# LN1 output transposed by the DMA engines, and its passes laid out anew: an encoder block on eight cores

## The reference

```
x   = _layernorm(ALPHA * x + mix, ln1_g, ln1_b)        # x1, (tokens, 1024)
hid = square(relu(einsum('bsd,df->bsf', x, w_ff1)))    # (tokens, 4096)
ffn = einsum('bsf,fd->bsd', hid, w_ff2)
x   = _layernorm(ALPHA * x + ffn, ln2_g, ln2_b)
```

## Time and profile before

| | before |
|---|---|
| median of 3 runs | 1169.84 us (1169.5 to 1170.7) |
| profiled execution, its time | 1169.95 us |
| its span (first to last instruction, slowest core) | 1168.4 us; the eight cores 1162.7 to 1168.4 us |
| TensorE busy | 1135.6 us (97% of the span), 5594 matmuls |
| VectorE / ScalarE / GpSimd busy | 520.6 / 272.6 / 140.8 us |
| mean granted TensorE clock | 0.995 |

### The profile page before, as it was taken

The page is one execution under the profiler, slowest core; times in us unless marked ns, Lnnn a source line. Parts: engine busy times, 40 slices in busy tenths (PEclk is TensorE's granted clock), DMA queues, the critical chain, the costliest instruction groups (busy, mean ns, idle before and its releaser), DMA issues.

```text
span 1168.4 us, 15456 instructions; the slowest of 8 cores (1162.7 to 1168.4 us)
## 1 busy us (share of the span) xinstructions
PE 1135.6 (97%) x5594; PEld 521.7 (45%) x5594; DVE 520.6 (45%) x741; ACT 272.6 (23%) x417; POOL 140.8 (12%) x259
## 2 busy tenths in 40 slices
PE   6999999999999999999999999999999999999996
PEld 2544444444444444444444444444444444444442
DVE  0554465322248434503188445642222854442347
ACT  1224422211125333100011343221111443330000
POOL 4002200000011010100120121000000101000012
PEclk9999999999999999999999999999999999999998
DMA  9986776355552484764447438544334307444402
GB/s 131 179 139 121 141 134 112 48 81 81 91 90 46 66 125 74 111 120 75 73 85 180 105 88 169 104 83 76 63 66 81 60 0 124 83 83 73 73 37 108
DMA packets 30602, 110.36 MB, mean 94 GB/s; under 512 B 3648, under 2 KB 4160, under 8 KB 30016
## 3 DMA queue, kind: packets, MB, share of 16 engines
q0 software_dynamic: 24624, 88.36, 46.9%
q1 hardware_dynamic: 5904, 21.02, 5.9%
HBM read 189.33 MB, written 8.39 MB: 169 GB/s over the span
## 4 chain that ended last, share of the span: by engine, by line
PE 83%; DMA 8%; DVE 4%; issue 3%; ACT 1%; POOL 1%; DVEq 0%; ACTq 0%; SPq 0%; POOLq 0%
PE ps L263 83%; DMA ring<-wblk 4%; DMA t<-bsrow 2%; DMA xhTs<-xhT 2%; DVE regQ L757 1%; DVE regQ L834 1%; ACT regP L761 1%; POOL ring L144 1%; DVE regP L509 0%; PE ps L266 0%; DVE t L492 0%; POOL regR L144 0%; DVE t L504 0%; ACT t L488 0%; DVE Cc L472 0%
## 5 line engine op out<-in xcount | busy, mean ns | idle before, releaser
L263 PE MATMUL ps<-regR,ring 128*128 128x512 bf16 x2944 | 661.8, 379 | 14.2 <-DMA regR<-xT 7.0
L263 PEld LDWEIGHTS ps<-regR,ring 128*128 128x128 bf16 x2944 | 285.4, 98 | 354.8 <-issue 22.4
L263 PE MATMUL ps<-ring,regP 128*128 128x512 bf16 x1024 | 221.3, 379 | 0.9 <-ACT t L805 0.9
L144 POOL DMA_DIRECT2D ring<-wblk x145 | 77.5, 540 | 770.7 <-PE ps L263 766.7
L263 PEld LDWEIGHTS ps<-ring,regP 128*128 128x128 bf16 x1024 | 100.1, 98 | 122.0 <-issue 1.4
L263 PE MATMUL ps<-regP,ring 128*128 128x512 bf16 x640 | 148.6, 379 | 0.0
L806 DVE TENSOR_TENSOR regP<-t 128x512 bf16<-128x512 f32 x128 | 88.2, 692 | 124.7 <-ACT t L805 124.5
L805 ACT ACTIVATE t<-ps 128x512 f32<-128x512 f32 x128 | 76.0, 597 | 134.4 <-PE ps L263 129.6
L263 PEld LDWEIGHTS ps<-regP,ring 128*128 128x128 bf16 x640 | 62.6, 98 | 75.5
L844 DVE SCALAR_TENSOR_TENSOR regQ<-regQ,ps 128x512 f32<-128x512 f32 x32 | 22.0, 688 | 133.8 <-PE ps L263 133.8
L503 ACT ACTIVATE t<-ps 128x512 f32<-128x512 f32 x48 | 28.3, 600 | 204.7 <-PE ps L263 195.2
(11 more groups left out here) (63 smaller groups left out, 591.6 us busy)
## 6 DMA issues: line engine op xcount, KB each, us to landing
ring<-wblk POOLq DMA_DIRECT2D x129, 512.0 KB, 7.6
bigW<-wbig POOLq DMA_DIRECT2D x4, 2048.0 KB, 21.1
regQ<-x SPq DMA_DIRECT2D x16, 512.0 KB, 5.5
y<-regQ SPq DMA_DIRECT2D x16, 512.0 KB, 3.0
ring<-wblk POOLq DMA_DIRECT2D x16, 384.0 KB, 9.8
regR<-xT POOLq DMA_DIRECT2D x8, 256.0 KB, 13.5
regR<-xT POOLq DMA_DIRECT2D x4, 512.0 KB, 14.1
t<-ln1g SPq DMA_DIRECT2D x2, 512.0 KB, 8.8
```

The costliest lines, as they stand in the source:

```text
L144: self.items.append(lambda e, out=out, in_=in_, sem=sem: e.dma_start(out=out, in_=in_).then_inc(sem, 16))
L263: return lambda e: e.matmul(out, lhsT=l, rhs=r, start=st, stop=sp_)
```

## The change

The PE transposes and the ScalarE copies of `tail` are gone, and with them the identity matrix that GpSimd made at the start. In their place `xbf(tt)` does the affine pass and then a transfer issued by SyncE that transposes while it copies, from the bf16 buffer in SBUF to `x1Tb` in SBUF. Each of the 8 transfers has its own semaphore. The negative mean moves from VectorE to ScalarE. The passes are laid out in two lists: `early`, what is done ahead of each head, and `late`, three pieces done after the 1st, 4th and 7th group of `stage_F1` (before: 3rd, 6th and 9th). Tile 5's affine pass and tile 6's `mid`, which stood ahead of the last head, are among the late ones now.

```diff
@@ -253,17 +251,14 @@
                 tick()
             return tok
 
-        def DMA(q, out, in_, semst, reads=(), writes=()):
+        def DMA(q, out, in_, semst, reads=(), writes=(), transpose=False):
             q.wait(deps(reads, writes))
-            tok = q.dma(out, in_, semst)
+            tok = q.dma(out, in_, semst, transpose)
             commit(tok, reads, writes)
             return tok
 
         def mm(out, l, r, st, sp_):
             return lambda e: e.matmul(out, lhsT=l, rhs=r, start=st, stop=sp_)
-
-        def tr(out, in_):
-            return lambda e: e.transpose(out=out, in_=in_, identity=identb[:])
 
         bankB = [Buf() for _ in range(8)]
         cur = [0]
@@ -356,6 +351,7 @@
         bbB = [[Buf(), Buf()] for _ in range(8)]
         zB = [[Buf(), Buf()] for _ in range(8)]
         x1bB = [Buf() for _ in range(8)]
+        x1b_sem = [[semaphore(f"x1b{i}"), 0] for i in range(8)]
         hidB = [[Buf(), Buf()] for _ in range(32)]
         memB = Buf(accum=True)
         colvB = Buf(accum=True)
@@ -451,8 +447,6 @@
             DMA(pool, xhT[:], xh_d, sem_xh, writes=[xhTB])
             for i in range(3, NS):
                 issue(i)
-            OP(pool, lambda e: e.memset(identb[:], 0.0), writes=[memB])
-            OP(pool, lambda e: e.affine_select(out=identb[:], in_=identb[:], compare_op=ALU.not_equal, fill=1.0, base=0, pattern=[[-1, 128]], channel_multiplier=1), reads=[memB], writes=[memB])
             OP(pool, lambda e: e.memset(ones[:], 1.0), writes=[memB])
             OP(pool, lambda e: e.memset(chalf[:], -0.5), writes=[memB])
             load_big(0)
@@ -756,7 +750,7 @@
                 r3 = rq[tt].rearrange("p (a b) -> p a b", a=2)
                 OP(dve, lambda e: e.scalar_tensor_tensor(out=r3, in0=r3, scalar=ALPHA, in1=ps[:, b0:b0 + 2, :], op0=ALU.mult, op1=ALU.add, accum_out=s1[:, 0:1]),
                    reads=[bankB[b0], bankB[b0 + 1], rqB[tt]], writes=[rqB[tt], st1B[tt]])
-                OP(dve, lambda e: e.tensor_scalar(out=s1[:, 1:2], in0=s1[:, 0:1], scalar1=-1.0 / D, scalar2=None, op0=ALU.mult),
+                OP(act, lambda e: e.activation(out=s1[:, 1:2], in_=s1[:, 0:1], func=AF.Copy, scale=-1.0 / D),
                    reads=[st1B[tt]], writes=[st1B[tt]])
                 OP(act, lambda e: e.activation(out=junk, in_=rq[tt], func=AF.Square, bias=s1[:, 1:2], accum_out=s1[:, 2:3]),
                    reads=[rqB[tt], st1B[tt]], writes=[junkB, st1B[tt]])
@@ -769,29 +763,23 @@
                    reads=[rqB[tt], st1B[tt], g1.B], writes=[rqB[tt]])
                 OP(pool, lambda e: e.tensor_tensor(out=s1[:, 4:5], in0=s1[:, 3:4], in1=chalf[:, 0:1], op=ALU.pow), reads=[st1B[tt], memB], writes=[st1B[tt]])
 
-            def tail(tt):
-                ts_ = slice(tt * 128, (tt + 1) * 128)
-                xb = xbt[tt % 3]
-                b0 = nb()
-                PEG([tr(psb[:, b0, kc, :], xb[:, kc * 128:(kc + 1) * 128]) for kc in range(8)],
-                    reads=[xbB[tt % 3], memB], writes=[bankB[b0]], do_tick=False)
-                OP(act, lambda e: e.activation(out=x1Tb[:, :, ts_], in_=psb[:, b0, :, :], func=AF.Copy), reads=[bankB[b0]], writes=[x1bB[tt]])
-
-            def step(k):
-                if 0 <= k - 3 < 8:
-                    tail(k - 3)
-                if 0 <= k - 2 < 8:
-                    affine(k - 2, xbt[(k - 2) % 3], xbB[(k - 2) % 3], b1)
-                if 0 <= k - 1 < 8:
-                    mid(k - 1)
-                if k < 8:
-                    head(k)
+            def xbf(tt):
+                affine(tt, xbt[tt % 3], xbB[tt % 3], b1)
+                DMA(sp, x1Tb[:, :, tt * 128:(tt + 1) * 128], xbt[tt % 3], x1b_sem[tt], reads=[xbB[tt % 3]], writes=[x1bB[tt]], transpose=True)
+
+            early = [[], [(mid, 0)], [(xbf, 0), (mid, 1)], [(xbf, 1), (mid, 2)], [(xbf, 2), (mid, 3)], [(xbf, 3)], [(mid, 4)], [(xbf, 4), (mid, 5)]]
+            late = [[(xbf, 5), (mid, 6)], [(xbf, 6), (mid, 7)], [(xbf, 7)]]
+
+            def run(ops):
+                for f, tt in ops:
+                    f(tt)
 
             for k in range(8):
-                step(k)
+                run(early[k])
+                head(k)
             if st + 1 < ST:
                 load_big(0)
-            return [lambda k=k: step(k) for k in range(8, 11)]
+            return [lambda ops=ops: run(ops) for ops in late]
 
         def f1_group(st, fc, half):
             i1 = plan[st]["F1"][fc // 2]
@@ -813,7 +801,7 @@
                 for fc in (2 * g, 2 * g + 1):
                     f1_group(st, fc, 0)
                     n += 1
-                    if n % 3 == 0 and drain:
+                    if n % 3 == 1 and drain:
                         drain.pop(0)()
             flush_deferred()
             for g in range(G0):
```

More of the change, by code:

```diff
@@ L139, in run_nomark, with dma @@
         self.items.append(lambda e, fn=fn: fn(e))
-    def dma(self, out, in_, semst):
+    def dma(self, out, in_, semst, transpose=False):
         semst[1] += 16
         sem = semst[0]
-        self.items.append(lambda e, out=out, in_=in_, sem=sem: e.dma_start(out=out, in_=in_).then_inc(sem, 16))
+        self.items.append(lambda e, out=out, in_=in_, sem=sem: e.dma_start(out=out, in_=in_, transpose=transpose).then_inc(sem, 16))
         return (sem, semst[1])
@@ L184, in build_program @@
         wsTb = sb("wsTb", [128, 8, 128], BF16)
-        identb = sb("identb", [128, 128], BF16)
         ones = sb("ones", [128, 128], F32)
@@ L206, in build_program @@
         junk = regP[:, 31744:32768]
-        psb = ps[:].rearrange("p b n -> p (b n)").bitcast(BF16).rearrange("p (b k n) -> p b k n", b=8, k=8)
         pe = Q("pe", semaphore("s_pe"))
```

## The result

| | before | after |
|---|---|---|
| median of 4 runs | 1169.67 us | 1156.12 us |
| profiled execution | 1169.95 us | 1155.04 us |
| its span | 1168.4 us | 1153.5 us |

The ratio of after to before is 0.9882, 95% interval 0.9868 to 0.9896: 13.8 us less. The forecast was 8.3 us less and 1161.5 us. One of the four executions of the changed kernel ran with the cores of one die at a lower clock and is left out of the ratio; the median of the three others is 1155.91 us, just under the stated range.

A forecast was written before the change was run, and what follows sets the result against it. TensorE, busy 97% of the span, was taken as the bound. 13.2 us removed, less waits of 2.2 and 2.5 and 0.2 for the mean, gave 8.3 us less, 1161.5 us; likeliest range 1157 to 1167, full range 1156 to 1184.

The forecast's parts named there:

- What bounds the kernel, and what the removal gives: TensorE bounds; removing transposes and their waits at heads and first FFN groups gives 6.6 us a super-tile, 13.2 at most.
- the four bank pairs: At the heads, VectorE falls 1 us a tile behind TensorE, but four PSUM bank pairs cover it.
- The mean on ScalarE: On the way to tile 3, moving the mean from VectorE to ScalarE was counted as +0.1 us.
- The wait for tile 3: At the first FFN group, a 5.5 us transfer, hidden to 3.3 and 3.0 us, makes TensorE wait 2.2 and 2.5 us.
- The high end: Upper bound on a transfer's duration: 64 rows an engine at 0.144 us, 9.2 us, so 10.6 us in all.
- the transfer is hidden: Rival at tile 3: up to 3.2 us from affine to landing, no wait, 13.2 us gained, 1156.6 us; chance 0.17.
- The two pages: On the transfer's cost: one implies nil wait and 13.2 us gained, the other 10.5 us for eight blocks one after another.
- Tiles 4 to 7: At the seventeenth FFN group, tile 7 has 9 us for its transfer: hidden, up to twice the taken duration.
- The slower rival: Transfers queue, tile 3 and the seventeenth FFN group come late: 1218 us, 1224 with clock loss; chance 0.27.
- S: Time in us that one transposing transfer occupies the DMA engines; above 4.42 us a queue forms.
- Its turn at S = 5.4: At tile 3, with queued transfers, the change turns from gain to loss at S = 5.4 us.

The follow-up runs named there:

- a1: The changed kernel with the passes in the old order and the negative mean back on VectorE: 1154.35 us, ratio to before 0.9883.
- a2: The changed kernel with only the negative mean back on VectorE: 1154.90 us, ratio to before 0.9884.
- a3: The kernel before with only the negative mean moved to ScalarE: 1167.16 us, ratio to before 0.9987.
- b3: The changed kernel with a plain copy in rows of 256 bytes for each transposing transfer, FFN input left untransposed: 1155.18 us, ratio to before 0.9890.
- b1: The changed kernel with every transposing transfer issued twice, the extra one first into an unused buffer: 1158.58 us, ratio to before 0.9922.
- c1: The changed kernel with every transfer issued four times and super-tile 1's `bigW` load moved ahead of the last part of `stage_F1`: 1177.14 us, ratio to before 1.0078.
- b2: The changed kernel with every transposing transfer issued four times, three of them into unused buffers: 1196.95 us, ratio to before 1.0252.
- a4: The kernel before with each set of TensorE's transposes one step later, no transfers: 1174.61 us, ratio to before 1.0055.

## Why the prediction was wrong, point by point

- **What bounds the kernel, and what the removal gives: right.** 13.2 us was the most that the change could give; the two stretches gave 12.9, and a1 shows that the transfers alone, without the new order and the mean, bring all of the gain. The measured 13.8 us is above this most by less than its interval (12.2 to 15.4). The heads stand in one row of 27.8 us, as said. VectorE falls behind and is covered by the four bank pairs.
- **The mean on ScalarE: no effect on the time of this kernel (a2), but the sign was wrong.** I counted 0.1 us a super-tile as lost; the affine pass of tile 3 comes 0.4 us earlier than in a2. Without the transfers the time falls by 1.5 us (a3), of which the two stretches show 0.7.
- **The wait for tile 3: the step that failed.** The place was right, and the margin nearly (3.3 and 3.0 us said, 3.7 measured in both super-tiles). The duration was not: "I take 5.5 us", measured 3.0 and 3.7. The waits were put at 2.2 and 2.5 us and were nil and 0.2. This term holds 4.5 of the 5.5 us by which the forecast missed; of the rest 0.2 is the mean, and some 0.9 lies outside the two stretches. The high end multiplied the time of a 4 KB packet, 0.144 us, with the number of 256-byte rows; a packet of 256 bytes costs 0.021 us. With it the duration is 1.4 + 64 x 0.021 = 2.7 us, near the measured one. That is the rival "the transfer is hidden", with 1156.6 us, to which I gave 0.17. It had the row of the idle engines on its side, and I chose a row taken amid traffic for a moment that the table of stretches showed empty.
- **The two pages.** The section X-Bar Transpose (TRN2) of the Trainium skill, "Advanced Engine Details and Errata", says that transposing transfers are as fast as ordinary ones; b3 agrees to within 0.1 us to landing, though not in the engines' time (1.37 against 1.15 us), if the ordinary one has rows of 256 bytes too. The 1,309 ns a block in "VectorE: DVE Perf Modes" of the Trainium skill, The three transpose paths, cannot be multiplied by eight: eight blocks in one transfer take 1.37 us of the engines and 3.0 us in all.
- **Tiles 4 to 7: right in the outcome, and partly by luck.** I put the cover of tile 7 at 9 us and any transfer at 5.5. Beside `bigW` tile 5's took 12.1 and tile 6's 8.6, which I had not seen coming; tile 7's took 3.1, but SyncE could not issue it until 2 us after its affine pass. They land with the load's end, and that end decides: 5.7 us ahead of TensorE here, 0.8 us too late in b1.
- **The slower rival** has the right shape: with four transfers in place of one, S is 5.5 and tile 3 comes late. Its turn at S = 5.4 does not hold: at 5.5 the kernel is already 9 us slower (c1), so the turn lies between b1, two transfers of 1.37 us and still faster than before, and c1; no run shows where.

## What to carry to other kernels

A transfer that nobody waits for replaces work of TensorE and the copy behind it, and what decides is the time from the last producer to the first consumer, here 3.7 us against a transfer of 3.0 to 3.7. Price a transfer of short rows by a row of like packets on engines equally busy, not by packets sixteen times as long. And look at what loads on the other queue at that moment: here a big load in long packets held up transfers of short ones until it was through (b2, c1), which costs nothing only as long as its end lies ahead of the consumer.

## What the runs showed of the hardware

- A transposing transfer of 128 x 1024 bf16 from SBUF to SBUF, alone: 1,056 packets, 1.37 us of the 16 engines, 3.0 us to landing, 1.23 us of SyncE's queue to issue. The plain copy in rows of 256 bytes (b3): 1,040 packets, 1.15 us, 2.9 us, 0.59 us.
- Two queues on the same engines went packet by packet where both had work: in b2 from 364 to 374 us as many of 16 KB as of 256 bytes in each 2 us, 103 beside 93 in 12 us. In the changed kernel a transfer of 3.0 us became 12.1, and in b2 SyncE's queue stood for some 15 us.
- A gap of 3.4 us in TensorE was followed by 3 us at a granted clock of 0.56 and, in the other super-tile, by 6 us at 0.50 (a4); after those of 24 and 12 us (b2, c1) it stood at 0.50.
